# Hybrid layer on one core: five sets of seven products instead of four, and the first set's weight sums made in memory

## The reference, cut to what matters

```python
h = rms_norm(x, ffn_norm_g[layer])
x = x + (jax.nn.silu(h @ w_ffn_gate[layer]) * (h @ w_ffn_up[layer])) @ w_ffn_down[layer]
return rms_norm(x, final_norm_g)
```

## Time and profile before

| | |
|---|---|
| median of three runs | 377.73 us (377.39 to 377.97) |
| the profiled execution | 377.2 us, its span 375.4 us |
| granted clock of PE over the span | 0.995 |
| PE busy | 367.1 us, 98% |
| DVE busy | 321.5 us, 86% |
| ACT busy | 230.7 us, 61% |
| POOL busy | 41.4 us, 11% |
| read from memory | 73.46 MB, 198 GB/s over the span |

### The profile page before, as it was taken

How to read it: one execution, slowest core, us unless ns; L and a number is a source line. 1 busy time by engine, 2 the same in 40 slices (tenths; PEclk the granted TensorE clock), 3 DMA queues, 4 the chain that set the end, 5 groups by cost and what they waited for, 6 DMA issues and landing times.

```text
span 375.4 us, 4744 instructions
## 1 busy us (share of the span) xinstructions
PE 367.1 (98%) x1847; PEld 309.0 (82%) x1847; DVE 321.5 (86%) x372; ACT 230.7 (61%) x267; POOL 41.4 (11%) x41
## 2 busy tenths in 40 slices
PE   7999999999999999999999999999999999999993
PEld 6998888788888888888888888888888888888882
DVE  4989987989867999989769669999999999999525
ACT  5767787676265956645447436955782892878205
POOL 2798020000000104000100000100100100000002
PEclk9999999999999999999999999999999999999998
DMA  8997255945270493899717902794796599360002
GB/s 284 282 296 266 60 182 207 320 143 210 57 281 0 66 345 120 321 353 308 281 55 276 358 39 55 179 384 172 184 359 236 129 308 347 113 248 33 0 2 112
DMA packets 41293, 74.80 MB, mean 199 GB/s; under 512 B 2316, under 2 KB 14648, under 8 KB 41272
## 3 DMA queue, kind: packets, MB, share of 16 engines
q1 hardware_dynamic: 38944, 70.03, 53.2%
q0 software_dynamic: 2112, 4.19, 6.6%
q10 hardware_dynamic: 216, 0.28, 0.2%
HBM read 73.46 MB, written 1.05 MB: 198 GB/s over the span
## 4 chain that ended last, share of the span: by engine, by line
PE 95%; DMA 1%; DVE 1%; issue 1%; POOL 0%; ACT 0%; POOLq 0%; SPq 0%; DVEq 0%; ACTq 0%
PE pp L1685 12%; PE pp L1687 12%; PE pp L1686 12%; PE pa L2069 7%; PE pa L2067 7%; PE pa L2068 7%; PE pp L1676 4%; PE pp L1665 3%; PE pp L1678 2%; PE pa L1676 2%; PE pa L2012 2%; PE pa L2010 2%; PE pa L1685 2%; PE pa L1687 2%; PE pa L2011 2%; PE pa L1686 2%
## 5 line engine op out<-in xcount | busy, mean ns | idle before, releaser
L1088 DVE TENSOR_TENSOR w_lo<-w_raw,w_hi 128x2048 fp32r<-128x2048 f32 x33 | 75.3, 2293 | 10.2 <-ACT w_hi L697 10.1
L970 ACT ACTIVATE w_hi<-w_raw 128x2048 fp32r<-128x2048 f32 x33 | 62.7, 1908 | 24.3 <-DVE w_raw L1536 24.3
L1556 DVE TENSOR_TENSOR w_lo<-w_raw,w_hi 128x2048 fp32r<-128x2048 f32 x33 | 74.6, 2283 | 0.2 <-ACT w_hi L970 0.2
L697 ACT ACTIVATE w_hi<-w_raw 128x2048 fp32r<-128x2048 f32 x33 | 62.6, 1912 | 19.6 <-DMA w_raw<-in_w_in 9.2
L1685 PE MATMUL pp<-w_hi,yT_hi 128*128 128x512 f32 (+1 forms) x104 | 40.5, 390 | 0.0
L1687 PE MATMUL pp<-w_lo,yT_hi 128*128 128x512 f32 (+1 forms) x104 | 40.3, 388 | 0.0
L1686 PE MATMUL pp<-w_hi,yT_lo 128*128 128x512 f32 (+1 forms) x104 | 40.3, 387 | 0.0
L1685 PE MATMUL pp<-w_hi,hT 128*128 128x512 f32 x96 | 38.0, 396 | 0.0
L1687 PE MATMUL pp<-w_lo,hT 128*128 128x512 f32 x96 | 37.4, 390 | 0.0
L1686 PE MATMUL pp<-w_hi,hT 128*128 128x512 f32 x96 | 37.4, 389 | 0.0
L2067 PE MATMUL pa<-w_hi,hT 128*128 128x512 f32 x64 | 24.9, 389 | 0.0
(11 more groups left out here) (341 smaller groups left out, 780.5 us busy)
## 6 DMA issues: line engine op xcount, KB each, us to landing
w_raw<-in_w_in SPq DMA_DIRECT2D x20, 1024.0 KB, 5.4
w_raw<-in_w_ffn_gate SPq DMA_DIRECT2D x11, 1024.0 KB, 8.9
w_raw<-in_w_ffn_up SPq DMA_DIRECT2D x11, 1024.0 KB, 8.5
w_raw<-in_w_ffn_down SPq DMA_DIRECT2D x11, 1024.0 KB, 7.9
w_raw<-in_w_o SPq DMA_DIRECT2D x4, 1024.0 KB, 5.3
x_sb<-in_w_ffn_gate POOLq DMA_DIRECT2D x3, 1024.0 KB, 9.3
w_raw<-in_w_out_attn SPq DMA_DIRECT2D x2, 1024.0 KB, 9.8
w_raw<-in_w_out_mlstm SPq DMA_DIRECT2D x2, 1024.0 KB, 5.2
```

The costliest lines, as they stand in the source:

```text
L697: nc.scalar.activation(w_hi[:, slot_of(c), :], early_raw(c), ACT.Copy).then_inc(hi_ready, 1)
L970: nc.scalar.activation(w_hi[:, slot_of(c), :], form_raw(name, p), ACT.Copy).then_inc(hi_ready, 1)
L1088: nc.vector.tensor_tensor(w_lo[:, slot_of(c), :], early_raw(c), w_hi[:, slot_of(c), :].bitcast(F32), ALU.subtract).then_inc(lo_ready, 1)
L1556: nc.vector.tensor_tensor(w_lo[:, slot_of(c), :], form_raw(*FORM[c]), w_hi[:, slot_of(c), :].bitcast(F32), ALU.subtract).then_inc(lo_ready, 1)
```

## The change

- There are five sets and one plain stretch: 5 x 512 + 256 = 2816. Set 0 has dN of the plain stretch behind its T3, and no product of hidden rows behind its B22.
- The four weight sums of set 0 are no longer made by DVE and in `x_sb`. During the attention POOL copies a chunk from memory to memory (`form_copy`, into the new tensor `formed`), and then adds a second one to it in memory (`form_grow`). The order is T1 = B12 + B11, T3 = B22 + B12, T2 = B22 + T1, T4 = B21 + T2; T1's pair stands ahead of POOL's mask of the mLSTM weights, the other three behind it and ahead of the adding transfer of the gate block. Each waits for a count of `lo_ready` (`STEP`), for its own copy and for the sum before. POOL's adding transfer for set 0 is gone.
- SP loads T1, T3 and T4 of set 0 like other chunks; T2 goes into `x_sb`, once the normed rows there have been transposed (`turned` 16), and SP waits for that ahead of the loads behind it.
- DVE has no split between the last split of the activations and the sums of the activations; `hS` and `third` are made earlier, ahead of the splits of B22,0 and T3,0.
- The splits run four chunks ahead instead of five, and three from T1,0 to T4,0's predecessor.
- Three semaphores are merged with others.

```diff
-SETS = 4
-PLAIN = 3
+SETS = 5
+PLAIN = 1
 SUMS = ("T1", "T2", "T3", "T4")
+AHEAD_FORMED = {("T1", 0): ("B12", "B11"), ("T3", 0): ("B22", "B12"), ("T2", 0): ("B22", ("T1", 0)), ("T4", 0): ("B21", ("T2", 0))}
+STORED = {form: n for n, form in enumerate(AHEAD_FORMED)}
+STEP = {("T1", 0): (5, 6), ("T3", 0): (14, 15), ("T2", 0): (16, 17), ("T4", 0): (18, 19)}
...
-    names = [("NG", 0), ("NU", 0), ("NG", 1), ("NU", 1), ("dN", 0), ("NG", 2), ("NU", 2)]
+    names = [("NG", 0), ("NU", 0)]
     for p in range(SETS):
-        before, after = (("dN", 1), ("dN", 2)) if p == 0 else (("dA", p - 1), ("dB", p - 1))
...
+        before, after = ([], [("dN", 0)]) if p == 0 else ([("dA", p - 1)], [("dB", p - 1)])
...
     if c < AT["NU", 0]:
         return C_SETS + 1
-    if c < AT["NU", 1]:
-        return AT["B11", 0] - 1
-    if c < AT["dN", 0]:
-        return AT["B11", 0]
-    first = AT["B11", 0]
-    ahead = RING if c < first else LEAD
+    ahead = LEAD - 1 if c <= AT["B11", 0] else LEAD - 2 if c < AT["T4", 0] else LEAD - 1
     return min(max(c + ahead, split_to(c - 1)), C_FFN + len(AT) - 1)
...
+    formed = nc.dram_tensor("formed", (len(STORED), P, CH), F32, kind="Internal").ap()
...
                 sp.dma_start(as_source(raw_of(buf), src), src).then_inc(chunk_loaded[buf], 16)
+                if (name, p) == ("B22", 0):
+
+                    src = ffn_source("T2", 0)
+                    sp.wait_ge(formed_grown, 16 * (STORED["T2", 0] + 1))
+                    sp.wait_ge(turned, 16)
+                    sp.dma_start(as_source(x_sb[:, :], src), src).then_inc(t2_loaded, 16)
...
+            def form_copy(name, p):
+
+                dst = formed[STORED[name, p]].rearrange("p (k n) -> p k n", k=4)
+                pool.wait_ge(lo_ready, STEP[name, p][0])
+                nc.gpsimd.dma_start(dst, ffn_source(AHEAD_FORMED[name, p][0], p)).then_inc(formed_copied, 16)
+
+            def form_grow(name, p):
+                second, n = AHEAD_FORMED[name, p][1], STORED[name, p]
+                dst = formed[n].rearrange("p (k n) -> p k n", k=4)
+                src = ffn_source(second, p) if isinstance(second, str) else ffn_source(*second)
+                pool.wait_ge(lo_ready, STEP[name, p][1])
+                pool.wait_ge(formed_copied, 16 * (n + 1))
+                if n:
+                    pool.wait_ge(formed_grown, 16 * n)
+                nc.gpsimd.dma_start(dst.rearrange("p k n -> k p n"), src.rearrange("p k n -> k p n"), accum_op=ALU.add
+                                    ).then_inc(formed_grown, 16)
+
+            form_copy("T1", 0)
+            form_grow("T1", 0)
             pool.wait_ge(w_exp_done, 2 * H_M)
...
+            form_copy("T3", 0)
+            form_grow("T3", 0)
+            form_copy("T2", 0)
+            form_grow("T2", 0)
+            form_copy("T4", 0)
+            form_grow("T4", 0)
             pool.wait_ge(lo_ready, GM["T2"] + 1)
             pool.wait_ge(gm_summed, 3)
...
-            for p in range(SETS - 1):
+            for p in range(1, SETS - 1):
                 pool.wait_ge(lo_ready, AT["T2", p] + 1)
                 pool.wait_ge(w_summed, sum_count("T3", p))
...
-            norm(3, gain_ffn)
-            turn_lo(7, 1, (pp[:, 0, :], pp[:, 1, :]))
-            split_lo(C_FFN + 3)
-            dve.wait_ge(h_copied, 1)
...
             plain(0, 0)
             plain(0, 1)
-            plain(1, 0)
-            plain_turn(0)
-            plain(1, 1)
-            down("dN", 0)
-            plain_turn(1)
-            plain(2, 0)
-            plain(2, 1)
             for p in range(SETS):
                 own, other = own_bank(p), 1 - own_bank(p)
                 if p:
                     pe.wait_ge(set_silu, 2 * p - 1)
+                else:
+                    pe.wait_ge(h_summed, 4)
                 product("B11", p, own, *quarter(0, 0), True)
...
                 product("B22", p, other, *summed(2), False)
-                if p == 0:
-                    down("dN", 1)
-                else:
+                if p:
                     down("dA", p - 1)
...
                 product("T3", p, own, *third, False)
                 if p == 0:
-                    down("dN", 2)
+                    down("dN", 0)
```

More of the change, by code:

```diff
@@ L66, in places @@
 def places():
-    names = [("NG", 0), ("NU", 0), ("NG", 1), ("NU", 1), ("dN", 0), ("NG", 2), ("NU", 2)]
+    names = [("NG", 0), ("NU", 0)]
     for p in range(SETS):
-        before, after = (("dN", 1), ("dN", 2)) if p == 0 else (("dA", p - 1), ("dB", p - 1))
-        names += [("B11", p), ("T1", p), ("T2", p), ("B22", p), before, ("T3", p)]
-        names += [after, ("B21", p), ("T4", p)] if p + 1 < SETS else [("B21", p), ("T4", p), after]
+        before, after = ([], [("dN", 0)]) if p == 0 else ([("dA", p - 1)], [("dB", p - 1)])
+        names += [("B11", p), ("T1", p), ("T2", p), ("B22", p)] + before + [("T3", p)]
+        names += after + [("B21", p), ("T4", p)] if p + 1 < SETS else [("B21", p), ("T4", p)] + after
     names += [("dA", SETS - 1), ("dB", SETS - 1)]
@@ L77, with grown @@
 AT = places()
-C_SETS = C_FFN + 4
+C_SETS = C_FFN + 3
 def lo_place(name, p):
     return 2 * AT[name, p]
+def grown(name, p):
+    return name == "T4" and 0 < p < SETS - 1
+SUMMED = [(name, p) for p in range(SETS) for name in SUMS if not grown(name, p) and (name, p) not in STORED]
 def sum_count(name, p):
-    return 3 * p + SUMS.index(name) + 1
-def grown(name, p):
-    return name == "T4" and p + 1 < SETS
+    return SUMMED.index((name, p)) + 1
 def sums_ahead(name, p):
-    return {"T1": ("T1", "T2"), "T2": ("T3",), "B21": ("T4",) if p + 1 == SETS else ()}.get(name, ())
+    sums = {"T1": ("T1", "T2"), "T2": ("T3",), "B21": ("T4",)}.get(name, ())
+    return [part for part in sums if (part, p) in SUMMED]
 FORM = {c: form for form, c in AT.items()}
@@ L142, in landings @@
             place("B11", p, "T3")
-            place("B12", p, "T1")
+            place("T1" if ("T1", p) in STORED else "B12", p, "T1")
             place("B22", p, "B22")
-        elif name not in SUMS + ("B22",):
+        elif (name, p) == ("T1", 0):
+            place("T1", p, "T1")
+            place("B22", p, "B22")
+        elif name not in SUMS + ("B22",) or (name, p) in (("T3", 0), ("T4", 0)):
             place(name, p, name)
@@ L330, in form_raw @@
         def form_raw(name, p):
-            if name in ("T2", "T4"):
+            if name == "T2" or name == "T4" and p:
                 return x_sb[:, :]
-            return raw_of(LANDED[{"T1": "B12", "T3": "B11"}.get(name, name), p][0])
+            if name in SUMS and (name, p) not in STORED:
+                name = {"T1": "B12", "T3": "B11"}[name]
+            return raw_of(LANDED[name, p][0])
         def plain_banks(n):
@@ L995, in _ @@
             nc.scalar.activation(sum2, pp[:, 1, :], ACT.Copy).then_inc(h_copied, 1)
-            form_hi(C_SETS)
+            act.wait_ge(h_summed, 4)
+            nc.scalar.activation(hS[:, 0, :, :].rearrange("p f n -> p (f n)"), region_a[:, 0:1536], ACT.Copy
+                                 ).then_inc(hS_hi_set, 1)
             form_hi(C_SETS + 1)
```

115 lines of the change are left out of this document (53 added, 62 removed).

## The result

The changed kernel takes **443.31 us** (442.57 to 444.45, four runs) against 377.69 (377.39 to 377.97) of the kernel before: 1.174 times as long [1.1712, 1.1768]. The forecast was 377.8, with a range up to 384.0. The loss is 65.6 us, and the profiled span grows from 375.4 to 442.7. Medians leave out a run that is more than 1.5% above the fastest of the same kernel; this concerns one run of e7.

What follows compares the result with a forecast made beforehand. TensorE, busy 98% of the span, was taken as the bound, VectorE close behind. Saving 2.7, waits 2.9, less 0.1 covered, memory work 0: +0.1 on 377.2, plus 0.5 from profiled to median, 377.8 us; range 375.0 to 384.0.

Steps and rivals of the forecast that it cites:

- the length of an accumulation in memory: GpSimd's four accumulating transfers for set 0: 10 us each, from the 9.3 us row of an accumulation into SBUF.
- the work in memory: GpSimd's four copies (7 us each) and four accumulations (10 us each), done in time for the gate block's transfer: cost 0.
- rival 3: Accumulations run on 4 of 16 engines, delaying the gate block's T4: +33, 411 us, up to 440 with loads; chance 0.18.
- Its chain: In rival 3, accumulations of 28 us each from 82.5, the last ending at 166.5, the gate block's transfer at 173.
- Rival 2: Slow accumulations in GpSimd's queue ahead of the gate block's; from 16 us each the kernel is slower, 384 at 18; chance 0.10.
- Rival 4: Loads of set 0 land late past their cover, T2's wait holding SyncE: 1 to 3 us more, 378.6 to 381; chance 0.10.
- The walk through the feed-forward block: From B11,0 on: twelve matmuls less save 2.7 us, VectorE's lateness makes TensorE wait 2.9 us in total.
- the wait at B11,1: Set 1 of the feed-forward block: TensorE waits 1.3 us with the handover, ended by ScalarE's silu.
- the wait at T2,1: Set 1 of the feed-forward block: TensorE waits 1.5 us more, until VectorE's split is ready at 239.75.
- T1,1 to T1,2: Distance between the T1 products of sets 1 and 2 on TensorE: some 32.5 us, later sets 30.8.
- VectorE's gap before dN,0: VectorE gets dN,0 at 217.3 after some 1.3 us without work, then has no gap.
- The block as a whole: Feed-forward block: 2.7 us saved, 2.9 us of waits, less 0.1 for slower matmuls they cover: +0.1.

Runs made afterwards that it cites:

- e7: Changed kernel with the gate block's transfer issued ahead of T2's and T4's accumulations in GpSimd's queue, accumulations still with 4 outermost; 421.85 us, 1.118 times the kernel before.
- e1: Changed kernel with the memory sums stored as 512 rows and each accumulating transfer with 16 outermost instead of 4; 377.45 us, ratio 0.9998 to the kernel before.
- e5: As e1 (sums stored as 512 rows), but each accumulating transfer takes every fourth row together, 4 outermost; 444.04 us, single run.
- e8: e1 with the split of dN,0 on ScalarE moved ahead of the copy of T2,0 out of its bank; 375.91 us, ratio 0.9965.
- e3: Changed kernel without the four copies and four accumulations in memory, set 0 reading plain weight blocks instead; 377.51 us, ratio 1.0002.
- e6: Changed kernel with only T1's accumulation at 4 outermost, the other three taking every sixteenth row, 16 outermost; 388.46 us, ratio 1.0295.
- e4: As e1 (sums stored as 512 rows), but each accumulating transfer takes every eighth row together, 8 outermost; 400.08 us, single run.

## Why the prediction was wrong

**The step that failed is the length of an accumulation in memory.** It was taken as 10 us from the nearest row, an accumulation into SBUF; measured were 36.0, 34.0, 33.5 and 24.4, and the cost of the work in memory, put at 0, was the whole loss. That row fits for the same work on the same 16 engines (10.4 in e1). It does not fit the pattern in the diff, which puts k outermost, and the row's own pattern has 128 partitions there. Both were known: rival 3 names the place, the mechanism and a way to price it, and got a chance of 0.18 and a seat outside the range. "No run here shows it" was treated as evidence against. It was only the absence of evidence, while the diff alone tells the two patterns apart.

**Rival 3's own sum** had the right parts and was half the size: 33 us, "up to 440" with the loads. Its 24.8 us for a chunk on four engines was right: T4's accumulation, without loads beside it, took 24.4. Its chain was not. It let the gate block's transfer land at 173, and it landed at 201.4, 28.4 later:

- The first accumulation holds up the loads, so T3's goes out at 96.62, not 82.5: 14.1.
- The next two follow 38.3 and 37.0 us apart, not 28: 19.3. The accumulation ahead took some 34 each time, and the copy queued behind it landed 3.8 and 2.8 us after it. The sum of the chain had left the copies out.
- T4's took 24.4, not 28, and the gate block's landed 5.0 behind it, not 6.5: 5.1 less.

It also counted from the wrong product. It set the end against T4's at 144.24, but TensorE stopped at T3's, at 138.80 before, since the copy for that product stands on ScalarE behind the split that waited. So 65.0 us were lost there, and 2.4 more up to B11,0, most of it in the matmuls at half the clock (0.43 us each until 208.7).

**Rival 2** (slow in itself) fell with e1 and e5. **Rival 4** (the loads of set 0): in e1 ScalarE waits for no load in set 0.

**The walk through the feed-forward block held.** It can be read in the changed kernel too, since everything there is only shifted. TensorE's timeline there: first the wait at B11,1, then T1,1's first matmul, the wait at T2,1, and the first matmuls of T1,2 and T1,3:

```profile
299.51 0.50 PE L2097 MATMUL pa<-w_hi,hT 128*128 128x512 f32 x1 [0.93 <-ACT region_a L1078]
...
302.41 0.39 PE L2097 MATMUL pa<-w_hi,hS 128*128 128x512 f32 x1
...
307.37 0.47 PE L2097 MATMUL pa<-w_hi,hS 128*128 128x512 f32 x1 [1.21 <-DVE w_lo L1586]
...
334.89 0.39 PE L2097 MATMUL pa<-w_hi,hS 128*128 128x512 f32 x1
...
365.72 0.39 PE L2097 MATMUL pa<-w_hi,hS 128*128 128x512 f32 x1
```

- No wait before B11,1; then one ended by ScalarE's silu, forecast 1.3 us, measured 0.93; then one ended by VectorE's split, forecast 1.5, measured 1.21.
- T1,1 to T1,2: forecast 32.5 us, measured 32.48. The next set: forecast 30.8, measured 30.83.
- VectorE's gap before dN,0: forecast 1.3, measured 1.13 in e1. e8 shows it as the cause of the wait at B11,1; the one at T2,1 stays when the gap is closed.
- The block as a whole: forecast 0.1 longer, measured 0.17 shorter. The waits were sized 0.8 us too long (2.9 against 2.1), which should have made the block 0.6 shorter; the other 0.4 isn't accounted for.
- With the accumulations on 16 engines the kernel takes 377.45 us; the forecast was 377.8, "no change", and that is what e1 and e3 show. That it comes so close is in part luck, as two misses of 0.8 and 0.4 us work against each other.

So the part with the most steps was right to some tenths, and the part costed in one sentence decided the result.

## What to carry to other kernels

For each new transfer write down the size of its outermost dimension, on both sides, before taking a price from another transfer's row; under 16, multiply (here by 1.9 with 8 and by 3.3 with 4). A transfer that nobody waits for still has a price when it sits on a few engines, since every load needs those too, and so does every copy queued behind it: here one such sum cost 11 us. And where a rival rests on something that the diff itself shows, it can't be left outside the range because no row of before shows it.

## What was not expected of the hardware

- Beside an accumulation on four engines a load of 1 MB lands every 8.2 us (e6, e7), against 2.7 in the same run once the accumulation has landed (e6: 78.02 to 80.75). The accumulation itself goes from 24.4 us to 33.5 to 36.0, and to 40.5 in e7, where it was issued right behind the gate block's transfer.
- A whole transfer in GpSimd's queue behind one on four engines is held up by it: the gate block's took 28.3 us in the changed kernel, 10.3 before, and 27.3 behind one on eight engines (e4). The plain copies behind one took 33.7 and 35.2, against 7.0 and 8.3 without.
- While TensorE had no work its granted clock stood at 0.50, the 1.2 GHz level, and came back to 1.00 only after work had begun again at 203.85. Windows of the changed kernel, with TensorE's busy time first, the granted clock and the DMA share near the end:

```profile
160.00:200.00 40.00, 0.00 (x0) 0.00 (x0) 0.00 (x0) 0.00 (x0) 3.33 (x2) 0.50 0.39 72
200.00:210.00 10.00, 6.15 (x17) 4.88 (x18) 5.62 (x16) 7.10 (x7) 0.00 (x0) 0.56 0.03 5
210.00:220.00 10.00, 10.00 (x47) 8.21 (x46) 9.97 (x17) 5.26 (x6) 3.87 (x2) 1.00 0.57 191
```

- Those 40 us also show that the mean DMA share misleads: 0.39, and yet a transfer was what everything waited for. Before 170 and after 185 us it stood at the level of four busy engines (0.27 and 0.28).
